# Two chained blocks in one kernel: modulation units moved to VectorE in the RWKV loop, gates by padded weights, constant products at the norms, and the residual's x read in four places

## What is computed

```python
mod = (silu(c) @ w_ada + b_ada)[:, None, :]
sh1, sc1, g1, sh2, sc2, g2 = jnp.split(mod, 6, axis=-1)
h = rms_norm(x, norm_mix) * (1.0 + sc1) + sh1
x = x + g1 * mixer(h, ...)
h = rms_norm(x, norm_ffn) * (1.0 + sc2) + sh2
x = x + g2 * conv_glu_ffn(h, w_ffn_up, conv_w, conv_b, w_ffn_down)
```

## Time and profile before

| | us |
|---|---|
| median of 3 runs | 2596.79 |
| lowest and highest | 2593.6, 2600.73 |
| the profiled execution, its own time | 2595.51 |
| its span, first to last instruction | 2593.7 |
| TensorE busy | 2509.9 (97%) |
| VectorE, ScalarE, GpSimd busy | 1401.5, 1123.8, 1223.9 |
| mean granted clock of TensorE | 0.982 |
| read from memory | 607.72 MB |

### The profile page before, as it was taken

How to read it: one execution, slowest core, us unless ns; L and a number is a source line. 1 busy time by engine, 2 the same in 40 slices (tenths; PEclk the granted TensorE clock), 3 DMA queues, 4 the chain that set the end, 5 groups by cost and what they waited for, 6 DMA issues and landing times.

```text
span 2593.7 us, 50406 instructions
## 1 busy us (share of the span) xinstructions
PE 2509.9 (97%) x19824; PEld 2292.8 (88%) x19824; DVE 1401.5 (54%) x2323; ACT 1123.8 (43%) x1316; POOL 1223.9 (47%) x500
## 2 busy tenths in 40 slices
PE   7999999989999999999998999999999999999997
PEld 5887887888999999998887977889999999998886
DVE  2535225455777777775665445345675766443333
ACT  2253324334544444444444344444544444444443
POOL 2663444666444444434443565557344444444442
PEclk9999999999999999999999899999999999999999
DMA  9963544687677777777767365458556565555553
GB/s 397 391 240 152 197 196 196 251 308 277 238 269 276 281 267 259 271 260 263 288 254 263 120 246 195 187 227 309 187 219 251 205 234 200 179 193 186 187 195 121
DMA packets 140382, 611.69 MB, mean 236 GB/s; under 512 B 15584, under 2 KB 15968, under 8 KB 115680
## 3 DMA queue, kind: packets, MB, share of 16 engines
q1 hardware_dynamic: 140256, 609.88, 64.0%
HBM read 607.72 MB, written 2.10 MB: 235 GB/s over the span
## 4 chain that ended last, share of the span: by engine, by line
issue 46%; PE 32%; POOL 20%; DVE 1%; POOLq 1%; DMA 0%; ACT 0%; DVEq 0%; SPq 0%; ACTq 0%
PE psum L1922 32%; POOL wlo L1731 20%; DVE xT L2244 0%; DMA ada_raw<-adastream 0%; POOLq L1728 0%; POOLq L1730 0%; PE psum L2138 0%; DVE psum L2244 0%; DVE gslo L2236 0%; ACT arena L1745 0%; ACT whi L1742 0%; ACT gshi L1742 0%; DVE arena L2338 0%; POOLq L1731 0%; ACT arena L1742 0%
## 5 line engine op out<-in xcount | busy, mean ns | idle before, releaser
L1731 POOL TENSOR_TENSOR wlo<-raw,whi 128x1024 fp32r<-128x1024 f32 x496 | 1223.7, 2472 | 1341.0 <-ACT whi L1742 1340.6
L1742 ACT ACTIVATE whi<-raw 128x1024 fp32r<-128x1024 f32 x760 | 802.0, 1061 | 985.7 <-PE psum L1922 744.3
L1922 PE MATMUL psum<-hi_h,whi 128*128 128x256 f32 x4224 | 1211.6, 287 | 15.0 <-issue 8.6
L1922 PE MATMUL psum<-hi_h,wlo 128*128 128x256 f32 x4224 | 1195.6, 283 | 0.0
L1922 PE MATMUL psum<-lo_h,whi 128*128 128x256 f32 x4224 | 1195.0, 283 | 0.0
L1922 PEld LDWEIGHTS psum<-hi_h,whi 128*128 128x128 f32 x4224 | 804.3, 190 | 27.1 <-issue 14.2
L1922 PEld LDWEIGHTS psum<-hi_h,wlo 128*128 128x128 f32 x4224 | 804.4, 190 | 1.9 <-issue 1.7
L1922 PEld LDWEIGHTS psum<-lo_h,whi 128*128 128x128 f32 x4224 | 804.0, 190 | 0.0
L2236 DVE TENSOR_TENSOR wlo<-raw,whi 128x1024 fp32r<-128x1024 f32 x264 | 378.4, 1437 | 280.9 <-ACT whi L1742 280.9
L2244 DVE SCALAR_TENSOR_TENSOR psum<-ada_raw,cact,psum 128x256 f32<-128x256 f32 x702 | 287.5, 483 | 11.2 <-DMA ada_raw<-adastream 11.2
L1922 PE MATMUL psum<-whi,gshi 128*128 128x512 f32 x704 | 277.5, 394 | 3.8 <-DVE gslo L2236 3.5
(11 more groups left out here) (162 smaller groups left out, 1647.2 us busy)
## 6 DMA issues: line engine op xcount, KB each, us to landing
raw<-wstream SPq DMA_DIRECT2D x760, 512.0 KB, 4.6
ada_raw<-adastream SPq DMA_DIRECT2D x168, 1024.0 KB, 7.0
arena<-adastream SPq DMA_DIRECT2D x24, 1024.0 KB, 17.8
xT<-x_in SPq DMA_DIRECT2D x8, 512.0 KB, 6.9
y_out<-xT SPq DMA_DIRECT2D x4, 512.0 KB, 2.6
gs_pages<-tabs_in SPq DMA_DIRECT2D x2, 512.0 KB, 4.4
gs_pages<-rw_in SPq DMA_DIRECT2D x2, 512.0 KB, 7.9
tabs<-tabs_in SPq DMA_DIRECT2D x1, 482.0 KB, 8.7
```

The lines of the kernel that those rows point to most:

```text
L1731: nc.gpsimd.tensor_tensor(wlo[:, q, :], raw[:, q, :], whi[:, q, :].bitcast(F32), ALU.subtract).then_inc(sem.lo_ready, 1)
L1742: return nc.scalar.activation(out_, in_, ACT.Copy, scale=scale)
L1922: return nc.tensor.matmul(o, lhsT, rhs, start=start, stop=stop, skip_group_check=True)
```

## The change

Four things are changed; nothing of the result is left out.

1. **Loop units.** The eight modulation units `LOOP_UNITS` of the RWKV loop are made by VectorE with the new `loop_products`, two for each pair `t`: five products in each of the levels 1 to 3 (three ahead of the level's subtraction, two behind), one in level 4, and in level 5 four ahead and twelve behind. The last goes to `acc`, whose 128 partitions TensorE sums with `ones` in place of `sel`. `spot()` no longer makes these units, only finishes the one before, and stands after the first fill of a pair and after level 4; one fill moves from ahead of the 64x128 blocks to the end of the pair. SyncE issues every second of these units one slab earlier.
2. **Gates.** The gate weights are padded with zeros to 128 columns (`wgs`, in four pages of the arena) and become the weight side; h is streamed, 48 matmuls of 128x256. VectorE clears 128x4096 for it, ScalarE waits for that before its copy, and the gates come out as rows, so one transposing matmul is left of four. VectorE's steps after it work on 64 partitions by 256.
3. **Products of constants.** `keep_busy(n)` issues n fp32 matmuls of `ident` by `tabs`, 128x256, into a bank that nobody reads, at norms 1, 2 and 4: 5 (4 at norm 2) ahead of `sums(3)`, 2 ahead of the `sel` matmuls, 2 (3 at norm 2) ahead of the spreading ones, and 6 after.
4. **The residual's x.** The four reads of 512 KB go out at the slab places 8, 11, 17 and 24 of the output projection, each with a semaphore of its own, and residual g waits for its own only.

```diff
+LOOP_UNITS = (START_UNITS + 3, START_UNITS + 11)
 def by_pe(u):
-    return u < MIX_UNITS1[1] or MIX_UNITS2[0] <= u < MIX_UNITS2[1]
+    return u < LOOP_UNITS[0] or LOOP_UNITS[1] <= u < MIX_UNITS1[1] or MIX_UNITS2[0] <= u < MIX_UNITS2[1]
...
         first = spots[u - units[0] - 1] + 4 if u > units[0] else spot - 6
+        if LOOP_UNITS[0] <= u < LOOP_UNITS[1] and (u - LOOP_UNITS[0]) % 2:
+            first -= 1
...
                 scores_of(1, bank[6], 0, sem.sc2)
                 fill(1)
+
+                spot()
...
                     fill(1)
-                    if l == 2:
+                    if l == 4:
                         spot()
-                fill(1)
                 pe.wait_ge(sem.t_ready, 6 * t + 6)
...
                 ins.then_inc(sem.fh, 1)
-                spot()
+                fill(1)
...
-                    if l == 3:
-                        unit_rows()
+                    loop_products(*{1: (2 * t, 0, 3), 2: (2 * t, 5, 8), 3: (2 * t, 10, 13), 4: (2 * t, 15, 16),
+                                    5: (2 * t + 1, 0, 4)}[l])
                     dve.wait_ge(sem.d_done, 5 * t + l)
...
+                    loop_products(*{1: (2 * t, 3, 5), 2: (2 * t, 8, 10), 3: (2 * t, 13, 15), 4: (2 * t, 16, 16),
+                                    5: (2 * t + 1, 4, 16)}[l])
...
+            def loop_products(n, k0, k1):
+                u = LOOP_UNITS[0] + n
+                for kt in range(k0, k1):
+                    s, k = divmod(kt, 8)
+                    if k == 0:
+                        dve.wait_ge(sem.ada_landed[s], 16 * (u - START_UNITS + 1))
+                    w, c = ada_raw[:, s, k * 256:(k + 1) * 256], cact[:, kt:kt + 1]
+                    if kt == 0:
+                        dve.wait_ge(sem.ada_sum, u)
+                        ts(sums_of(0), w, c, None, ALU.mult).then_inc(*at.up(sem.step))
+                    else:
+                        dve.wait_ge(*st["sum"])
+                        at.n[sem.ada_used] = u
+                        stt(acc[:, 0, 0, :] if kt == KT - 1 else sums_of(0), w, c, sums_of(0), ALU.mult, ALU.add
+                            ).then_inc(*at.up(sem.ada_used if kt == 7 else sem.acc_ready if kt == KT - 1 else sem.step))
+                    st["sum"] = at.last
...
             pe.wait_ge(sem.wg_ready, 1)
-            for tb in range(2):
-                o = bank[5][:, tb * 16:(tb + 1) * 16]
-                t = slice(tb * P, (tb + 1) * P)
-                for kt in range(KT):
-                    w = slice(kt * 16, kt * 16 + 16)
-                    mm(o, hhi[:, kt, t], wg_hi[:, w], tb == 0 and kt == 0, False)
-                    mm(o, hlo[:, kt, t], wg_hi[:, w], False, False)
-                    ins = mm(o, hhi[:, kt, t], wg_lo[:, w], False, kt == KT - 1)
-                    if tb and kt == KT - 1:
-                        ins.then_inc(sem.gates, 1)
+            for kt in range(KT):
+                ins = product(bank[5][:, 0:S], wgs[:, 0, kt, :], wgs[:, 1, kt, :], hhi[:, kt, :], hlo[:, kt, :],
+                              kt == 0, kt == KT - 1)
+            ins.then_inc(sem.gates, 1)
...
+            ahead(0, 0)
             act.wait_ge(sem.tables2_landed, 48)
-            copy(wg_hi, small[:]).then_inc(sem.wg_hi, 1)
+            act.wait_ge(sem.wz0, 1)
+            copy(gate_columns(0), wg_in4).then_inc(sem.wg_hi, 1)
...
+            dve.wait_ge(sem.slab_used, B2)
+            V.memset(wgs[:].bitcast(F32), 0.0).then_inc(*at.up(sem.wz0))
...
+            tt(gate_columns(1), wg_in4, gate_columns(0).bitcast(F32), ALU.subtract).then_inc(*at.up(sem.wg_ready))
             unit_rows()
...
             dve.wait_ge(sem.gates, 1)
+            ts(gate_in, bank[5][:, 0:S], gate_bias, None, ALU.add).then_inc(*at.up(sem.step))
             dve.wait_ge(*at.last)
+            ts(f_min, gate_in[FORGET], 0.0, None, ALU.min).then_inc(*at.up(sem.step))
             dve.wait_ge(*at.last)
+            stt(f_abs, f_min, 2.0, gate_in[FORGET], ALU.mult, ALU.subtract).then_inc(*at.up(sem.f_abs))
             dve.wait_ge(sem.f_ln, 1)
+            tt(f_min, f_min, f_abs, ALU.subtract).then_inc(*at.up(sem.gt_ready))
...
+            def keep_busy(n):
+                for _ in range(n):
+                    mm(bank[4 if st["spare"] == 0 else 0][:, 0:S], ident, tabs[:, 0:S], True)
+
             def wide(N):
                 kinds = 4 if N == 2 else 2
+                if N < 5:
+                    keep_busy(2)
                 pe.wait_ge(sem.norm_dve, 2 * NORMS[N] - 1)
...
-            for k in range(4):
-                sp.dma_start(xT[:, 4 * k:4 * k + 4, :], x_in[:, 4 * k:4 * k + 4, :]
-                             ).then_inc(sem.x_landed, 16)
-            out_slabs(B1_OUT + GS, B1_UP, at_out)
+            out_slabs(B1_OUT + GS, B1_UP, at_out, {B1_OUT + GS + (0, 3, 9, 16)[k]: functools.partial(x_again, k) for k in range(4)})
...
-                    if g == 0 and n0 == B1_OUT:
-                        dve.wait_ge(sem.x_landed, 128)
+                    if n0 == B1_OUT:
+                        dve.wait_ge(sem.start_landed[g], 16 * START_UNITS // START_PAIRS + 16)
```

More of the change, by code:

```diff
@@ L119, in rows_made @@
 def rows_made(u):
[L121 to L122 removed]
+    assert by_pe(u), u
+    return sum(by_pe(v) for v in range(u + 1))
 def by_pe(u):
[L126 removed]
+    return u < LOOP_UNITS[0] or LOOP_UNITS[1] <= u < MIX_UNITS1[1] or MIX_UNITS2[0] <= u < MIX_UNITS2[1]
 def ada_places(n0, units, spots):
@@ L366, in __init__ @@
         self.wz = new("wz")
+        self.wz0 = new("wz0")
         self.x_landed = new("x_landed")
@@ L1178, in kept2, with gate_columns @@
             return 9 + ORDER2.index(name) + 1
-        wg_hi, wg_lo = gslo[:, 0, 0, :], gslo[:, 0, 1, :]
+        def gate_columns(part):
+            return wgs[:, part].rearrange("p k (g r) -> p k g r", r=32)[:, :, :, 0:4]
+        wg_in4 = small[:].rearrange("p (k g h) -> p k g h", g=4, h=4)
         dft = halves(19)
[L1182 to L1185, removed]
+        gate_bias = stat[:, 6:7]
+        gate_one = page(22)[:, 768:784]
+        FORGET = slice(64, 128)
+        gate_in = page(22)[:, 0:256]
+        f_min, f_abs = page(22)[FORGET, 256:512], page(22)[FORGET, 512:768]
         row_c, row_m, row_b, row_s = (tiles(14)[:, k, :] for k in range(4))
@@ L1197, in build, with pe_mix2 @@
         mask_f, mask_b = page(20)[:, S:2 * S], page(20)[:, 0:S]
-        def pe_mix2(pe, st, mm, part, spot):
+        def pe_mix2(pe, st, mm, product, part, spot):
             def slot(g, s):
@@ L1309, in pe_mix2 @@
             pe.wait_ge(sem.gt_ready, 1)
[L1310 to L1315, removed]
+            mm(bank[4][BOTH, 0:S], ident[FORGET, FORGET], f_min, True).then_inc(sem.rows_made, 1)
             slot(1, 2)
@@ L1621, in mixer, with out_slabs @@
                     slab(n)
-            def out_slabs(n0, n1, at):
+            def out_slabs(n0, n1, at, more=None):
                 for n in range(n0, n1):
+                    if more and n in more:
+                        more[n]()
                     if n in at:
@@ L1993, in finish_rows @@
                     c = sums_at + 2 * (start_unit_id(u) if u < START_UNITS else u) + j
-                    ins = mm(bank[7][:, c:c + 1], acc[:, b, 0, j * P:(j + 1) * P], tab("sel")[:, 0:1], j == 0)
+                    which = tab("sel")[:, 0:1] if by_pe(u) else ones[:, 0:1]
+                    ins = mm(bank[7][:, c:c + 1], acc[:, b, 0, j * P:(j + 1) * P], which, j == 0)
                     if j:
@@ L2010, in spot @@
                 u, (u0, u1), spots = st["unit"], st["units"], st["spots"]
-                assert u == u1 or st["slabs"] == spots[u - u0], (u, st["slabs"])
+                assert u == u1 or not by_pe(u) or st["slabs"] == spots[u - u0], (u, st["slabs"])
                 if u in st["after_taken"]:
@@ L2016, in spot @@
                 if u == u1:
+                    return
+                if not by_pe(u):
+                    st["unit"] += 1
                     return
@@ L2181, in down @@
                     turn(12, 2, (tb,))
-                for k in range(2, 4):
-                    sums(N, k)
+                st["spare"] = 1
+                sums(N, 2)
+                if N < 5:
+                    keep_busy(4)
+                sums(N, 3)
                 wide(N)
@@ L2222, in _ @@
             st.update(unit=MIX_UNITS2[0], units=MIX_UNITS2, spots=SPOTS2, slabs=0, after_taken={MIX_UNITS2[0]: 10})
-            pe_mix2(pe, st, mm, part, spot)
+            pe_mix2(pe, st, mm, product, part, spot)
             output(B2_OUT, MIX2, 4, 12, (sem.mix_split, 4, 2))
```

46 lines of the change are left out of this document (26 added, 20 removed).

## The result

| | median us | ratio to before, 95% interval |
|---|---|---|
| before | 2594.38 (2593.60 to 2600.73, 5 runs) | |
| changed | 2582.83 (2577.83 to 2585.50, 5 runs) | 0.9948 (0.9931 to 0.9965) |

The account below looks back on a forecast made before the run. TensorE, busy for 97% of the span with the weights' matmuls, was taken as the bound. Terms −12.7 −5.9 −0.6 −1.8 −12.0 −2.3 sum to −35.3, from 2595.5 to 2560.2, forecast as 2561 us; range 2551 to 2575.

Parts of the forecast that it names:

- The loop: RWKV pairs: TensorE is spared eight units, 14.7 us, less 2.0 of waits at the pairs' ends; sum −12.7 us.
- VectorE's last group: End of each RWKV pair: 12 products at 0.52 us, 6.2 us in all, from 255.3 to 261.5.
- the pair's end: RWKV loop: TensorE waits 0.5 us a pair before the next pair's scores, +2.0 us in all.
- The lead: SyncE's queue in the loop: being a few us ahead, it makes the shifted slab order cost nothing.
- Rival 4: Loop: late VectorE exposes SyncE's slab transfers, 11.6 us a pair; 2607 or 2596 us in total; chance 0.05.
- The x reload: Output projection: spreading x's four reads lands the modulation unit earlier, cutting the stall to about 0.7; −5.9 us.
- Rival 3: Output projection: the x reload moves nothing because the stretch is full of DMA; +5.9, 2567 us; chance 0.09.
- The gates: Gates: 48 wider matmuls replace 96, −11.2, clock kept −1.8, stall ahead +1.0; sum −12.0 us.
- The norms: Norms 1, 2 and 4: products of constants hold TensorE's clock; −0.6, −1.8 and −2.3 us.
- rival 1: Norms: the products of constants don't hold the clock and cost time; 2573 us; chance 0.12.
- the 0.95 wait: Up-projection after norm 1: its first sum already waits 0.95 us for VectorE, so only −0.6 of −1.4 was kept.
- The rule on two SBUF inputs: Gates: VectorE and GpSimd exclude each other, new steps cost some 1.8 us more, 2563; loop's products not concerned.

Follow-up runs that it names:

- k = 2: Changed kernel with the second half of every odd loop unit issued two slabs later on SyncE's queue: 2561.91 us, ratio 0.9865 to before.
- k = 1 to 3: Changed kernel with the second half of every odd loop unit issued one, two or three slabs later on SyncE's queue: 2561.21, 2561.91, 2561.77 us.
- the fastest version: k = 2 with the gates' matmuls two slabs later and ScalarE's gate-weight copy behind the next two slabs' copies: 2560.06 us, ratio 0.9848 to before.

## Why the prediction was wrong

1. **The loop: −12.7 forecast, +9.6 measured** (+7.2 by the medians). What was reckoned on TensorE and for VectorE's last group was right. The products took 0.482 in the mean, the last group ran from 251.06 to 257.38 in the kernel with k = 2, 6.3 us for 6.2; the pair's end cost 0.16 in place of 0.5, and the loop part gives 12 there. The step that failed is this sentence: "SyncE is a few us ahead there, so I cost it at nothing." The lead was taken from the kernel before, where it holds for another reason: TensorE uses up a unit in one go of 1.84 us, so both halves of `ada_raw` come free at once. On SyncE's queue before, only a slab that is free stands between the two halves:

```profile
241.37 0.33 SPq L1609 DMA_DIRECT2D ada_raw<-adastream  x1
241.74 0.43 SPq L1597 DMA_DIRECT2D raw<-wstream  x1
242.23 0.41 SPq L1609 DMA_DIRECT2D ada_raw<-adastream  x1
```

VectorE spreads the same unit over four levels, 17 us in the second pair, and holds the second half for the last ten of them, while SyncE's next request for that half stands one slab behind the request for the first, which comes free at the eighth product. The stall follows from the order of the two queues: letting one slab through first removes it. In the changed kernel it is made longer by a step of VectorE that the forecast did not have, up to 1.8 us a pair (point 7).
2. **Rival 4 was the right mechanism at the wrong place, with 0.05.** It made the stall hang on the last group of products ending over 5 us late; that group was on time in the kernel with k = 2. The stall sits at the first unit's last product, in level 4, and comes in every pair. Its price was 11.6 for a pair; measured were 3.5 of waiting (14.0 / 4) and 1.9 of half clock, 21.5 in four pairs by the slab times (14.2 won with k = 2, 7.3 lost without). TensorE worked on from slabs already split until 250.3, and I had not counted these; the rest of the 11.6 was covered by them.
3. **ScalarE's part was not in the prediction at all.** The price is paid first through its queue: the slab's copy stands ahead of the small one.
4. **The x reload: −5.9 forecast, −4 to −6 measured.** The wait fell from 4.33 to 0.56 (0.7 forecast), and the clock behind it stayed at 1.00. Rival 3, that a full DMA stretch moves nothing, fell: the share is 0.99 after the change too, only the order of what lands is another.
5. **The gates: −12.0 forecast, −11.5 to −12.2 measured.** The clearing took 3.47 us (3.6 forecast). But the stall was mis-sized: 2.93, and 2.8 of half clock behind it (the 48 matmuls took 8.5 us from 1454.67 in place of 5.7), where I took 1.0. The step that failed there is the start: VectorE came to the clearing only at 1450.11, after its modulated rows, not at 1444.5; the chain itself took 4.5 in place of 6.5. That the whole term held all the same is chance in part: the kernel with the old gates has a wait of 1.68 for modulated rows at slab 407 that k = 2 has not (seven long products in place of six).
6. **The norms: −4.7 forecast, −4.1 measured** on the kernel before, and not to be told from nothing in three pairs of kernels with and without (they are worth 0.6, −3.0 and 2.4 us by the medians). The clock at the norms is held as forecast: rival 1 fell, as the windows at 1.00 show. What the forecast lacked is who comes next. TensorE leaves norm 2 earlier and meets VectorE's modulated rows or gate weights, which are not earlier; one or two more of the modulated rows even fall beside a split and are longer. I had written this for norm 1 and the 0.95 wait (1.44 now), not for norm 2.
7. **The rule on two SBUF inputs** (the Trainium skill, SBUF — State Buffer, "SBUF: two separate sides") was weighed only for the gates and waved through for the loop, since a product reads one stream of SBUF. This case's trace agrees with it in both places. The gates' subtraction took 0.43 with GpSimd idle, where before it took 2.29; so it cost nothing there. But in the loop the multiplication of the mask, both inputs in SBUF, took

```profile
238.73 0.43 DVE L2269 TENSOR_TENSOR arena<-arena,tabs 128x256 f32<-128x256 f32 x1 [0.58 <-PE psum L1934]
```

with GpSimd idle and 2.20 at 243.60, beside GpSimd's split

```profile
243.14 2.38 POOL L1743 TENSOR_TENSOR wlo<-raw,whi 128x1024 fp32r<-128x1024 f32 x1 [5.49 <-ACT whi L1754]
```

The product behind it, the sixteenth, was held by that, and SyncE with it: 1.8 of its 9.7 us. It is so in all four pairs (2.20, 2.05, 1.82 and 2.07). What it adds is seen in the trace without the constants, where the loop is the same program but in the first pair the split began only at 244.33, behind the multiplication:

```profile
243.60 0.43 DVE L2269 TENSOR_TENSOR arena<-arena,tabs 128x256 f32<-128x256 f32 x1 [0.58 <-PE psum L1934]
243.94 0.47 DVE L2277 SCALAR_TENSOR_TENSOR acc<-ada_raw,cact,psum 128x256 f32<-128x256 f32 x1
```

```profile
252.00 0.68 PE L1934 MATMUL psum<-arena 64*64 64x64 f32 x16 [1.66 <-ACT arena L1754]
```

TensorE waited 1.66 there in place of 4.83 and kept the full clock; between slabs 41 and 72 that trace loses 2.4 us, not 7.3. With k = 2 the multiplication still takes 2.04 in the first pair and holds nobody.

The range, 2551 to 2575, missed. The 2561 in it is what a kernel with one other queue place takes (2561 to 2562 with k = 1 to 3). That the sum fits it so well is luck in part: the gates' term holds with the help of a wait of 1.68 in the kernel that it is measured against, and on the kernel with k = 2 the norms' term can't be told from nothing.

## What to carry to other kernels

When work moves from an engine that uses a buffer in one go to one that uses it in pieces, the buffer is held longer though no work is late. Look up the request that waits for it, and count what stands behind that request on the same queue: if it is the ring that feeds the busiest engine, count the slabs that come free while it waits. The same holds for a compute engine that waits for one product with copies behind it. And when a stage is made faster, ask what the engine meets next; a gain ends at the first wait for an engine that was not made faster.

## What the runs showed beside this

- The clock of TensorE after a wait is not the same from trace to trace. After a wait of 2.66 us with the same matmuls on both sides, eight matmuls took 1.99 in the kernel before and 3.38 in the fastest version:

```profile
1547.82 1.99 PE L1922 MATMUL psum<-gs_pages,arena 128*128 128x256 f32 x8 [2.66 <-DVE gs_pages L2236]
```

```profile
1512.40 3.38 PE L1934 MATMUL psum<-gs_pages,arena 128*128 128x256 f32 x8 [2.66 <-DVE gs_pages L2269]
```

  Each such place is worth 1.4 to 2.9 us by the slab times (the one at slabs 101 to 103 too), which is the size of most of the differences left. What decides between them was not tried, and one trace of each kernel can't tell whether it is the kernel or the execution.
- In the kernel before, the clock fell during the 96 matmuls of 128x16 though TensorE was busy all the time. With the fp32 matmuls of constants in the norms, whose waits add up to 6 us without them, it was at 1.00 behind each.
